# Where the four strips of inverted blocks are read back: all on SyncE's queue, or two on SyncE's and two on ScalarE's

## The reference

```python
kb = k * beta[..., None]
lmat = jnp.einsum('nbhcd,nbhed->nbhce', kb, k) * decay_strict
tmat = lax.linalg.triangular_solve(lmat + eye, jnp.broadcast_to(eye, lmat.shape),
                                   left_side=True, lower=True, unit_diagonal=True)
u_base = jnp.einsum('nbhce,nbhef->nbhcf', tmat, v * beta[..., None])
w_dec = jnp.einsum('nbhce,nbhed->nbhcd', tmat, kb * jnp.exp(gc)[..., None])
```

## Time and profile before

| | before |
|---|---|
| median of 3 runs | 1962.38 us (1961.54 to 1963.22) |
| the profiled execution | 1964.62 us |
| its span | 1962.8 us |
| PE busy | 1943.4 us (99% of the span) |
| DVE busy | 1347.8 us (69%) |
| ACT busy | 903.9 us (46%) |
| DMA, mean rate | 161 GB/s |

### The profile page before, as it was taken

One profiled execution on the slowest core, in us unless ns is written; L12 is line 12 of the kernel. 1 busy time (PEld: TensorE's weight loads), 2 busy tenths in 40 slices (PEclk: granted clock), 3 DMA queues, 4 the chain that ended last, 5 costly groups with the idle time before them and its releaser, 6 DMA issues.

```text
span 1962.8 us, 43764 instructions
## 1 busy us (share of the span) xinstructions
PE 1943.4 (99%) x15277; PEld 1892.0 (96%) x15277; DVE 1347.8 (69%) x2580; ACT 903.9 (46%) x1924; POOL 209.6 (11%) x356
## 2 busy tenths in 40 slices
PE   9999999999999999999999999999999999999998
PEld 8999999999999999999899999999999999999998
DVE  5899889898889888899544455545555556644443
ACT  6465555555565555555433443333333333433343
POOL 5210111111110111112000100000000000000010
PEclk9999999999999999999999999999999999999999
DMA  8555556655655556655544454444544454444443
GB/s 252 166 157 163 162 164 178 179 160 160 173 162 167 162 164 176 176 167 158 190 152 148 136 178 146 154 158 145 164 145 154 158 159 145 153 150 159 141 143 104
DMA packets 424841, 315.35 MB, mean 161 GB/s; under 512 B 63337, under 2 KB 421050, under 8 KB 424506
## 3 DMA queue, kind: packets, MB, share of 16 engines
q1 hardware_dynamic: 384280, 306.39, 51.3%
q10 hardware_dynamic: 40498, 8.14, 2.1%
HBM read 285.81 MB, written 29.55 MB: 161 GB/s over the span
## 4 chain that ended last, share of the span: by engine, by line
PE 52%; DVE 1%; DMA 0%; ACT 0%; issue 0%; ACTq 0%; DVEq 0%
PE ps L334 17%; PE ps L336 17%; PE ps L335 17%; PE ps L1407 0%; DMA x_blocks<-n 0%; PE ps L1968 0%; DVE wlo L321 0%; PE ps L2233 0%; PE ps L2257 0%; DVE xlo L1121 0%; DVE t L1214 0%; DMA xc<-x_blocks 0%; PE ps L1997 0%; DVE n L1206 0%; DVE lmat L1165 0%
## 5 line engine op out<-in xcount | busy, mean ns | idle before, releaser
L334 PE MATMUL ps<-xhi,whi 128*128 128x320 f32 x3072 | 976.8, 318 | 2.6 <-DVE zraw L1010 1.7
L336 PE MATMUL ps<-xhi,wlo 128*128 128x320 f32 x3072 | 949.6, 309 | 0.0
L335 PE MATMUL ps<-xlo,whi 128*128 128x320 f32 x3072 | 949.3, 309 | 0.0
L316 ACT ACTIVATE whi<-wraw 128x1024 fp32r<-128x1024 f32 x480 | 494.8, 1055 | 433.7 <-PE ps L336 290.5
L321 DVE TENSOR_TENSOR wlo<-wraw,whi 128x1024 fp32r<-128x1024 f32 x480 | 575.3, 1221 | 170.4 <-ACT whi L316 167.9
L334 PEld LDWEIGHTS ps<-xhi,whi 128*128 128x128 f32 x3072 | 577.3, 188 | 22.5 <-issue 14.1
L335 PEld LDWEIGHTS ps<-xlo,whi 128*128 128x128 f32 x3072 | 577.8, 188 | 0.9
L336 PEld LDWEIGHTS ps<-xhi,wlo 128*128 128x128 f32 x3072 | 577.2, 188 | 0.0
L334 PE MATMUL ps<-bhi,whi 128*128 128x320 f32 x512 | 158.2, 309 | 0.0
L335 PE MATMUL ps<-blo,whi 128*128 128x320 f32 x512 | 158.1, 309 | 0.0
L336 PE MATMUL ps<-bhi,wlo 128*128 128x320 f32 x512 | 158.1, 309 | 0.0
(11 more groups left out here) (369 smaller groups left out, 2008.4 us busy)
## 6 DMA issues: line engine op xcount, KB each, us to landing
wraw<-in_delta_w_in_dram SPq DMA_DIRECT2D x384, 256.0 KB, 3.2
wraw<-in_pool_w_in_dram SPq DMA_DIRECT2D x256, 256.0 KB, 3.2
wraw<-in_delta_w_out_dram SPq DMA_DIRECT2D x128, 256.0 KB, 3.4
wraw<-in_pool_w_out_dram SPq DMA_DIRECT2D x128, 256.0 KB, 3.2
s_s<-in_state_delta_dram SPq DMA_DIRECT2D x32, 512.0 KB, 5.3
out_dram<-s_s SPq DMA_DIRECT2D x32, 512.0 KB, 4.0
wraw<-in_pool_w_group_dram SPq DMA_DIRECT2D x64, 256.0 KB, 3.1
dec_in<-gc_rows SPq DMA_DIRECT2D x16, 320.0 KB, 4.0
```

Of the source, the lines that this page charges most:

```text
L316: nc.scalar.activation(whi[:, slot, :], wraw[:, slot, :], ACT.Copy).then_inc(E("w_hi"), 1)
L334: mm(o, whi[:, slot, w], hi[:, k_x, :], start=first, stop=False)
L335: mm(o, whi[:, slot, w], lo[:, k_x, :], start=False, stop=False)
L336: done = mm(o, wlo[:, slot, w], hi[:, k_x, :], start=False, stop=last)
```

## The change

SP issues all four strips. ACT issues none of them, and no longer waits for `x_out` at that place. The values, their places and the semaphore's count are the same.

```diff
         def strips_back(n):
 
             sp.wait_ge(E("x_out"), n * 16 + 16)
-            for h in range(2, 4):
+            for h in range(4):
                 sp.dma_start(xc[BL * h:BL * h + BL, :, :], strip_blocks(x_dram, h)).then_inc(E("x_in"), 16)
...
             act.dma_start(small_blocks(x_dram), n16[0:40, 0:256].rearrange("p (r c) -> p r c", c=16)).then_inc(E("x_out"), 16)
             split(5)
-            act.wait_ge(E("x_out"), n * 16 + 16)
-            for h in range(2):
-                act.dma_start(xc[BL * h:BL * h + BL, :, :], strip_blocks(x_dram, h)).then_inc(E("x_in"), 16)
             split(6)
             split(7)
```

## The result

| | before | changed |
|---|---|---|
| median (7 runs each, side by side) | 1963.22 us | 1969.72 us |
| ratio, 95% interval | | 1.0031 [1.0022, 1.0041] |
| the profiled execution: time, span | 1964.62, 1962.8 us | 1968.44, 1966.6 us |

The change makes the kernel slower by about 6 us; the forecast was 4.5 us. A second comparison gave 1.0027 [1.0016, 1.0038]. The two profiled spans differ by only 3.8 us, which has to be explained as well.

What follows compares the result with a forecast made beforehand. PE, busy for 99% of the span, was taken as the bound. Stalls of 2.7 (13 alike heads) + 0.74 (head 8) + 0.36 (head 1) + 0.67 (head 16) = 4.5 us on 1962.38 gave 1966.9 us, range 1963.0 to 1971.0.

Steps and rivals of the forecast that it cites:

- The fourth issue at t0 + 1.34: On SP, the fourth strip's issue starts 1.34 us after t0, the start of the head's first strip issue.
- The landing at 1.8 us after issue: The last SP strip lands 1.8 us after its issue, at t0 + 3.14; `yc` starts no earlier than t0 + 3.17.
- The loss of heads 2 to 15: PE stalls at `pc`: 0.21 us mean over 13 alike heads, 2.7 us, plus 0.74 us in head 8.
- Head 1 at 0.36 us: In head 1 PE already waits 0.80 us for `pc`, so DVE's 0.36 us lateness reaches PE whole.
- Head 16 at 0.67 us: In head 16 `yc` starts at t0 + 3.17 instead of t0 + 2.50, costing 0.67 us.
- The signal time of 0.14 us: From the end of `pc` on DVE to PE's start, 0.14 us is the cost of passing the signal.
- ACT's gain at nothing: In every head ACT's earlier `split(6)` gains nothing, as no reader waits for it.
- SP's loads of piece 10 at nothing: Loads queued behind SP's strips go some 0.8 us later but cost nothing; ACT reads that piece over 6 us after.
- Landing in time (1963.1 us): Rival: strips still land in time, `yc` could start at t0 + 2.80; loss 0.7 us, no change; chance 0.20.
- Slow landing: Rival: SP's strips land in 2.2 us, `yc` starts at t0 + 3.57; loss 11.0 us, 1973.4 us; chance 0.10.
- The second half-speed stretch: Rival: in head 16 PE's half-speed clock stretch comes twice, 1.7 us further, 6.2 us in all, 1968.6 us; chance 0.05.
- ACT's freedom: Rival: the freed ACT makes the kernel faster, by at most 0.3 us, 1962.1 us; chance 0.03.

Runs made afterwards that it cites:

- second profile: The changed kernel run once more, compared with the kernel before: ratio 1.0027 [1.0016, 1.0038], 1969.45 against 1963.97 us.
- the kernel with `pc` first: The changed kernel with DVE's update of `pc` ahead of `split(6)` instead of behind it: ratio 1.0003 [0.9994, 1.0012] to the kernel before.
- the kernel before with `pc` first: The kernel before (strips two and two) with DVE's update of `pc` ahead of `split(6)`: ratio 0.9997 [0.9988, 1.0006], 1963.01 against 1963.42 us.
- the five issues: The changed kernel with a spare transfer of strip 0 on SP ahead of the four: ratio 1.0065 [1.0052, 1.0079] to the kernel before.

## Why the prediction was right, and where its sizes were off

*The time.* Forecast 1966.9 us from a median of 1962.38, that is +4.5 us; measured +6 us, slower as forecast and within the range. The kernel before itself measured 1963.2 in the longer comparison.

*The fourth issue at t0 + 1.34:* right to the hundredth in head 16 (938.01 - 936.67). ACT's queue was a fair stand-in for SP's pace.

*The landing at 1.8 us after issue:* slightly short. It is the median of all strips; the fourth took 1.87 in head 16. `yc` started at t0 + 3.21 in head 6 and 3.23 in head 16, at 3.22 in the mean of heads 2 to 15, against my 3.17.

*The loss of heads 2 to 15:* the term that was mis-sized. I had 2.7 + 0.74 = 3.4 us; from head 2 to head 16 the changed kernel took 5.0 us more in its first profile and 4.0 us more in its second. Two steps make it up. DVE's lateness I had at 13 x 0.30 + 0.74 = 4.6 us; DVE's waits for the strips in these heads were 5.4 and 4.8 us. The larger miss is the slack: of this lateness I let about 0.09 us a head be hidden at `pc` (0.05 in head 2, 0.12 in head 15), 1.1 us in all, but nearly all of it reached PE in the first profile and 0.8 us less than all in the second. The two heads of the mean were not the fault: all 13, read in the same way from the trace of the kernel before, give 0.23 us a head where the two gave 0.21. The slack that they show in the kernel before was mostly not there any more in the changed one; why not, no run shows. Nor was the late `x_out`, which I booked as 0.74 us, a property of head 8: in the changed kernel's profile it is heads 3 and 13 whose strips wait longest for it (2.2 us from the write, where most heads have 2.0), and head 8 is like the others.

*Head 1 at 0.36 us:* the size is right, the place is not. In the second profile PE waits 0.42 us more there, but for `yc`, where it already waited 0.21 us before; its wait for `pc` stays at 0.80. The first profile can't speak of it: head 1 came early, PE waited 0.1 us there in all, and the 55.41 - 55.05 = 0.36 us more from head 1's strips to head 2's (156.17 - 101.12 = 55.05 before) are equal to my number by chance. *Head 16 at 0.67 us:* 0.55 in the first profile, 3.71 - 2.97 = 0.74 in the second.

*The signal time of 0.14 us, and that in heads 2 to 15 the stall goes through `pc` and not `yc`:* right; 0.15 us in head 6, and moving `pc` alone takes that loss away.

*ACT's gain at nothing:* right, shown twice, by its longer idle time ahead of L812 and by the kernel in which ACT waits as before. *SP's loads of piece 10 at nothing:* right for this kernel, as the kernel with `pc` first shows, in which they are as late. But the working had the wrong idea of them: I asked only whether the loads would be late, not whether the loads slow the strips. In the changed kernel all four strips are issued ahead of the load, which is the good order; the kernel with one strip on SP shows what the bad one costs, 17.7 us. The range would not have held that, and that the change has the good order is luck as far as the working goes.

*The rule that was weighed.* "DMA: Bandwidth & Descriptors" of the Trainium skill, section "Issuing engines are not separate DMA queues", says that spreading saves only the sequencers' time, usually small beside the transfer. The runs bear out that it saves this time; it is not small here, 0.34 to 0.44 us an issue against 1.8 us to the landing, and it makes the 6 us. The other half, that transfers of different engines interleave on the same DMA engines, agrees with the two kernels that have three strips on ACT: 2.9 us with a load of the other queue ahead, at most 2.1 without.

*Rivals.* Landing in time (1963.1 us) falls: all 15 heads wait. Slow landing falls for this kernel, though the one with three strips on ACT shows that it exists. The second half-speed stretch did not come in either profile of the changed kernel, but it is no empty rival: four other kernels show it (see the last section). ACT's freedom brought nothing.

## What to carry to other kernels

Count the issue time of small transfers that one instruction waits for: of four of 20 KB on one queue the last begins 1.34 us after the first, of two and two on two queues 0.40 us after it. Whether it matters is decided by the slack at the next meeting point with the bound engine, which one reads as the distance from the end of the helper's instruction to the start of the reader, less that distance where the reader is known to wait. Do not count on a tenth of a microsecond of slack read from one execution: here it was mostly gone in the next kernel. Issue the small transfers that somebody waits for ahead of the next large load, on whichever queue that stands. And if an engine's order is written by hand, look first whether the awaited instruction can go ahead of one that nobody waits for: here one line moved took back nearly all that the change had cost.

## What the runs showed of the hardware that was not expected

A 20 KB strip issued a quarter of a microsecond behind the start of a 256 KB load of the other queue landed in 2.8 to 3.0 us, one issued as much ahead of it in 1.8 to 2.3 us. Two useless strips that pushed the load back made the kernel 15 us faster.

A second thing: between two executions of the same program (the changed kernel) the first head's strips came 2.65 us apart, at 98.83 and at 101.48, so a span of 3.8 us more stood for a loss of about 6.

A third: the half-speed stretch in head 16 is not always 3.5 us long. It lasts 6.8 us in the profiles of the kernel before with `pc` first, of the five issues and of both kernels with three strips on ACT. In the first of these PE idled 2.7 us for `yc`, less than the 2.97 us of the kernel before with its short stretch, so the length of the idle time alone does not decide. What does is open. The first row is the stretch there, the second what follows it:

```profile
935.10:941.90 6.80, 6.31 (x82) 5.80 (x82) 4.61 (x11) 3.70 (x12) 0.00 (x0) 0.50 0.79 258
941.90:945.00 3.10, 3.10 (x54) 2.69 (x54) 0.01 (x1) 1.50 (x3) 0.00 (x0) 1.00 0.27 91
```
